# A two-block transformer on one core: modulation begun later, its sums kept in SBUF, activations saved in quarter tiles, side steps moved, four gate tiles

## The reference

```python
def _layer(x, ...):                      # first block, l = 0, 1
    proj = rms_norm(x, g_pre) @ w_in     # width 5952
    o_a = dense_attention(norm+rope(a_q), norm+rope(a_k), a_v) * silu(a_g)     # 8 heads of 128, 2 key heads
    o_b = dense_attention(q from norm(b_cq) @ w_uq, k, v from norm(b_ckv) @ w_ukv) * silu(b_g)   # 4 heads
    o_c = neighbourhood_attention(c_q, c_k, c_v, rpb) * silu(c_g)              # 4 heads, bias rpb
    return x + rms_norm(concat(o_a, o_b, o_c) @ w_out, g_post)

def hybrid_layer(x, c, ...):             # second block, l = 0, 1
    shift, scale, gate = split(silu(c) @ w_mod + b_mod)       # w_mod is 2048 x 6144
    h = rms_norm(x, g_pre) * (1 + scale) + shift
    a, s, g, z = split(h @ w_in)
    y = concat(sliding_window_attention(a), spatial_gating(s), gated_linear_attention(g)) * silu(z)
    return x + gate * rms_norm(y @ w_out, g_post)
```

## Time and profile before

| | |
|---|---|
| three runs | 3612.33, 3614.10, 3618.86 us (median 3614.1) |
| the profiled execution | 3606.72 us |
| its span in the profile | 3604.0 us |
| PE busy | 3484.3 us (97%), 17180 products |
| DVE busy | 1876.4 us (52%) |
| ACT busy | 1329.0 us (37%) |
| POOL busy | 1157.5 us (32%) |
| moved by DMA | 494.63 MB, 137 GB/s on average |
| PE on the chain that ended last | 83% |

### The profile page before, as it was taken

One profiled execution on the slowest core, in us unless ns is written; L12 is line 12 of the kernel. 1 busy time (PEld: TensorE's weight loads), 2 busy tenths in 40 slices (PEclk: granted clock), 3 DMA queues, 4 the chain that ended last, 5 costly groups with the idle time before them and its releaser, 6 DMA issues.

```text
span 3604.0 us, 47975 instructions
## 1 busy us (share of the span) xinstructions
PE 3484.3 (97%) x17180; PEld 2807.5 (78%) x17180; DVE 1876.4 (52%) x3156; ACT 1329.0 (37%) x2206; POOL 1157.5 (32%) x1244
## 2 busy tenths in 40 slices
PE   6999999999979999999999999999999999999998
PEld 5767878888766678788887878877887878877887
DVE  5633376543675334765436535645546535645545
ACT  5122323333541323333336535332236625423233
POOL 5664666664374546656620000002000000002000
PEclk9999999999989999999999999999999999999999
DMA  8644454455774444544556522322346622322345
GB/s 305 163 117 132 124 147 112 135 151 184 225 243 120 111 120 137 136 115 131 175 179 202 171 77 59 97 71 60 122 158 199 195 77 64 97 70 59 123 143 184
DMA packets 232384, 494.63 MB, mean 137 GB/s; under 512 B 36158, under 2 KB 45305, under 8 KB 226024
## 3 DMA queue, kind: packets, MB, share of 16 engines
q1 hardware_dynamic: 181352, 356.57, 32.8%
q0 software_dynamic: 33536, 109.10, 11.2%
q10 hardware_dynamic: 17280, 26.07, 2.3%
HBM read 470.58 MB, written 24.75 MB: 137 GB/s over the span
## 4 chain that ended last, share of the span: by engine, by line
PE 83%; DVE 8%; ACT 3%; DMA 3%; issue 2%; DVEq 0%; SPq 0%; ACTq 0%
PE bank L759 20%; PE bank L761 19%; PE bank L760 19%; PE bank L887 4%; PE bank L907 3%; DVE wlo L1699 2%; PE bank L873 2%; PE bank L754 2%; DMA stage<-in_w_out 2%; PE bank L756 2%; PE bank L755 2%; PE bank L896 2%; PE bank L1011 1%; DMA stage<-in_w_in 1%; PE bank L1143 1%
## 5 line engine op out<-in xcount | busy, mean ns | idle before, releaser
L759 PE MATMUL bank<-wlo,act_hi 128*128 128x512 f32 (+1 forms) x3712 | 1504.7, 405 | 71.4 <-DVE wlo L1699 60.4
L761 PE MATMUL bank<-whi,act_lo 128*128 128x512 f32 (+1 forms) x3712 | 1448.1, 390 | 0.0
L760 PE MATMUL bank<-whi,act_hi 128*128 128x512 f32 (+1 forms) x3712 | 1445.0, 389 | 0.0
L1699 DVE TENSOR_TENSOR wlo<-stage,whi 128x1024 fp32r<-128x1024 f32 (+1 forms) x624 | 831.3, 1336 | 880.8 <-ACT whi L1229 873.1
L1229 ACT ACTIVATE whi<-stage 128x1024 fp32r<-128x1024 f32 (+1 forms) x624 | 648.6, 1042 | 1029.2 <-PE bank L761 821.0
L759 PEld LDWEIGHTS bank<-wlo,act_hi 128*128 128x128 f32 x3712 | 702.9, 189 | 262.3 <-DVE wlo L1699 74.2
L761 PEld LDWEIGHTS bank<-whi,act_lo 128*128 128x128 f32 x3712 | 702.0, 189 | 148.8
L760 PEld LDWEIGHTS bank<-whi,act_hi 128*128 128x128 f32 x3712 | 704.2, 190 | 137.3 <-issue 7.7
L2648 POOL TENSOR_TENSOR macc<-macc,mprod 128x512 f32<-128x512 f32 x360 | 504.5, 1401 | 66.5 <-POOL mprod L2641 66.5
L2641 POOL TENSOR_SCALAR mprod<-wmod,csil 128x512 f32<-128x512 f32 x384 | 323.6, 843 | 378.7 <-DMA wmod<-in_w_mod 270.6
L2686 POOL DMA_DIRECT2D macc<-in_gla_w_gate_up x4 | 2.1, 528 | 1047.1 <-DVE Y L2297 1047.1
(11 more groups left out here) (259 smaller groups left out, 3222.6 us busy)
## 6 DMA issues: line engine op xcount, KB each, us to landing
stage<-in_w_in SPq DMA_DIRECT2D x400, 512.0 KB, 3.8
wmod<-in_w_mod POOLq DMA_DIRECT2D x384, 256.0 KB, 3.3
stage<-in_w_out SPq DMA_DIRECT2D x192, 512.0 KB, 4.1
out<-Y ACTq DMA_DIRECT2D x20, 1024.0 KB, 5.3
zone<-out SPq DMA_DIRECT2D x16, 1024.0 KB, 6.9
stage<-in_w_in SPq DMA_DIRECT2D x32, 320.0 KB, 4.0
Y<-in_x SPq DMA_DIRECT2D x4, 1024.0 KB, 13.7
rpb_tiles<-rpb_pad POOLq DMA_DIRECT2D x16, 224.0 KB, 5.9
```

Source lines behind the costliest of these rows:

```text
L759: pe.matmul(out, hi_x, lo_w, start=(k == 0), stop=False)
L760: pe.matmul(out, hi_x, hi_w, start=False, stop=False)
L761: mm = pe.matmul(out, lo_x, hi_w, start=False, stop=(k == KC - 1))
L1699: dve.tensor_tensor(wlo[:, c % RH, :, 0:width], stage[:, c % RS, :, 0:width], whi[:, c % RH, :, 0:width].bitcast(F32), ALU.subtract).then_ ...
```

## The change

1. **Modulation later.** In both layers POOL waits for the second increment of `prep` (the end of `key_rope_b`, step 36) before panel 0. Panels 0 and 1 now both stand ahead of the bias tiles. The sums of panels 0 to 3 move to steps 52, 62, 76 and 86 (`SUM_AT`; before 36, 52, 68, 84); those of panels 4 to 9 stay at steps 100 to 180, the last two at their places in the output sets. Attention units make room: branch B's 16 still end at step 68, branch C's begin at 81 (before 83) and end at 100 as before.
2. **Sums stay in SBUF.** `mrow` holds all 48 columns of both layers; ACT no longer writes to HBM at each sum. Shift and scale are used from there (`take_cols`); only the gate vectors go to HBM, by two DMAs of POOL, each 128 partitions by 16 numbers of 4 bytes (2048 numbers), when the first four head pairs of the sliding-window attention of the second block's first layer are done.
3. **Saves of x.** ACT saves no tile of x any more, except at the very end. SP saves in quarter tiles of 256 KB, one after each second weight cell, tile 0 in the last set of the layer before, tiles 1, 2, 3 in the layer's first, second and third set. The first layer saves nothing: its end reads `in_x`.
4. **w_uq and w_ukv in pieces.** SP loads `w_uq` in four DMAs in the fourth set and `w_ukv` in two in the fifth, in place of whole ones ahead of the third set.
5. **Start.** x's first tiles are loaded ahead of the small rows; ACT squares them ahead of the tangent of c, splits the first two weight cells ahead of the normalising, and normalises tile 0 while DVE normalises tile 1.
6. **Branch B's second latent** is squared and scaled in two halves (steps 24 and 33; before, both at 33). **Branch A's** key steps begin at 101 (before 107) and are spread to 112, its queries' to 113 to 122 and 134 to 148.
7. **Gates.** Four tiles in place of three, and DVE frees all four banks before it multiplies into Y.

```diff
-MOD_AT = {2: 0, 3: 1, 4: 2, 5: 3, 6: 4, 7: 5, 8: 6, 9: 7, 10: 8, 11: 9, 13: 10, 14: 11}
+MOD_AT = {6: 4, 7: 5, 8: 6, 9: 7, 10: 8, 11: 9, 13: 10, 14: 11}
-UNIT_TURN, UNIT_PV, ROW_SUM = 2, 4, 4
+UNIT_TURN, UNIT_PV = 2, 4
+SUM_AT = {52: 0, 62: 1, 76: 2, 86: 3} | {p * KC + 4: MOD_AT[p] for p in range(6, 12)}
-for first, steps in ((U_B, unit_steps(51, 16)), (U_C, unit_steps(83, 16))):
+for first, steps in ((U_B, unit_steps(51, 16)), (U_C, unit_steps(81, 16))):
+CKV0_AT = 24
-A_LOAD_AT, AK_AT, AQ_AT = 105, 107, (115, 131)
+A_LOAD_AT, AK_AT = 105, 101
+FOLD_AT, KROPE_AT = (112, 107), {108: 0, 109: 1, 110: 2, 111: 3}
+AQ_AT, ASUM_AT, ARSQ_AT = (113, 131), (116, 134), (122, 136)
+QROPE_A_AT = {113: (0, 0), 115: (0, 1), 119: (0, 2), 121: (0, 3), 139: (1, 0), 141: (1, 1), 146: (1, 2), 148: (1, 3)}
...
+            def x_save(blk, l, t, q):
+                def go():
+                    sp.wait_ge(x_new.sem, x_new.at(blk, l, t + 1 - TT))
+                    part = slice(q * PW, (q + 1) * PW)
+                    sp.dma_start(x_dram[:, t, part], Y[:, t, part]).then_inc(x_saved.sem, 16)
+                return go
...
-                in_set(0, l, 0, B_CQ0, first=4 if l == 0 else 0)
-                in_set(0, l, 1, B_CKV0, B_CKV_W)
-                sp.dma_start(wuq, io["b_w_uq"][bass.ds(l, 1)].rearrange("o (k p) n -> p (o k) n", p=P))\
-                sp.dma_start(wukv, io["b_w_ukv"][bass.ds(l, 1)].rearrange("o (k p) n -> p (o k) n", p=P))\
-                in_set(0, l, 2, B_CQ0)
-                in_set(0, l, 3, B_CKV0, B_CKV_W)
+                in_set(0, l, 0, B_CQ0, first=4 if l == 0 else 0, between=x_saves(0, l, 1))
+                in_set(0, l, 1, B_CKV0, B_CKV_W, between=x_saves(0, l, 2))
+                in_set(0, l, 2, B_CQ0, between=x_saves(0, l, 3))
+                in_set(0, l, 3, B_CKV0, B_CKV_W, between={2 * r + 1: w_uq(l, r) for r in range(4)})
...
             def mod_row_out(l, p):
                 act.wait_ge(mod_sum.sem, mod_sum.at(0, l, p + 1))
-                act.activation(mrow[:, :], MSUM[:, 0:PW // P], ACT.Copy).then_inc(mod_ev.sem, 1)
-                act.dma_start(mod_dram[bass.ds(l, 1), bass.ds(p * PW, PW)].rearrange("o (i c) -> c (o i)", c=P), mrow[:, :],
-                              allow_slow_non_contiguous=True).then_inc(mod_row.sem, 16)
+                act.activation(mrow[:, l, TT * p:TT * (p + 1)], MSUM[:, 0:PW // P], ACT.Copy).then_inc(mod_ev.sem, 1)
...
-                    gate(0)
-                    gate(1)
-                    apply(0)
-                    gate(2)
-                    apply(1)
-                    gate(3)
-                    apply(2)
-                    apply(3)
+                    for t in range(TT):
+                        gate(t)
+                    for t in range(TT):
+                        apply(t)
...
             for l in range(2):
-                pool.wait_ge(x_new.sem, x_new.at(0, l, -2))
+                pool.wait_ge(prep.sem, prep.at(0, l, CKV_READY + 1))
                 mod_panel(l, 0, 0)
+                mod_panel(l, 1, 1)
                 bias_tiles(l)
-                mod_panel(l, 1, 1)
...
+            pool.wait_ge(fin_done.sem, fin_done.at(1, 0, 4))
+            for l in range(2):
+                pool.dma_start(mod_dram[bass.ds(l, 1), :].rearrange("o (i c) -> c (o i)", c=P), mrow[:, l, 2 * KC:3 * KC],
+                               allow_slow_non_contiguous=True).then_inc(mod_row.sem, 16)
```

More of the change, by code:

```diff
@@ L60 @@
 U_B, U_C, U_A = 0, 16, 32
-UNIT_TURN, UNIT_PV, ROW_SUM = 2, 4, 4
+UNIT_TURN, UNIT_PV = 2, 4
+SUM_AT = {52: 0, 62: 1, 76: 2, 86: 3} | {p * KC + 4: MOD_AT[p] for p in range(6, 12)}
 GATED_STEPS = (2, 3, 4, 5, 6, 7, 8, 9, 10, 12, 14)
 def unit_steps(first, n, gates=False):
-    free = [s for s in range(first, first + 3 * n) if (s + UNIT_PV) % KC not in (ROW_SUM, ROW_SUM + 1)
+    free = [s for s in range(first, first + 3 * n) if s + UNIT_PV not in SUM_AT and s + UNIT_PV - 1 not in SUM_AT
             and (s < GATE0[0] * KC or not gates or s % KC in GATED_STEPS)]
@@ L437, in build, with sq_a @@
         tmp_a = view(ZT + 3584, 4, PW)
-        gate_tmp1 = [view(ZT + i * PW, PW) for i in range(3)]
+        gate_tmp1 = [view(ZT + i * PW, PW) for i in range(3)] + [view(ZV + 3 * PW, PW)]
+        def sq_a(half):
+            return (view(PP + 2048, 4, PW), tmp_a)[half]
         gain_at = ZK, ZT
@@ L563, in build @@
         gate_w, gate_b = macc[:, 0, 0:256], macc[:, 0, 256:512]
[L564 removed]
+        gate_tmp = (mprod[:, :], macc[:, 0, :], macc[:, 1, :], spare4[:, :])
         gsum, gmasks = view(PP, LEVELS + 2, P), view(PP + 1024, LEVELS + 2, P)
@@ L722, in _ @@
                 apart(sp)
-                spread(view(ZT, DM), mod_dram[one, 2 * DM:3 * DM], gain_in)
+                sp.wait_ge(mod_row.sem, mod_row.at(1, 2, 0))
+                apart(sp)
+                spread(view(ZT, DM), mod_dram[one, :], gain_in)
                 spread(view(ZV, DM), io["b_mod_2"][one, 2 * DM:3 * DM], gain_in)
```

246 lines of the change are left out of this document (137 added, 109 removed).

## The result

The changed kernel takes 3581.9 us (median of four runs, 3579.5 to 3584.1) against 3613.2 us (four runs of the kernel before, 3605.6 to 3618.9). The ratio is 0.9914, 95% interval 0.9894 to 0.9935: faster clear of the scatter, though by under 1%; 31 us by the medians, where the forecast had 16. The profiled execution is the one of 3579.51 us, 27.2 less than the profiled one before.

What follows compares the result with a forecast made beforehand. PE was taken as the bound, busy 97%, with only idle and half-clock time to win. Gains of 4 + 13 + 35 + 6 + 11 = 69 us less 53 us of waits for POOL gave -16: 3598 us, range 3562 to 3645.

Steps and rivals of the forecast that it cites:

- Start, 4: Kernel start to the first weight product: reordered splits, shared normalising and earlier x save 4 us (2 to 6).
- Steps 0 to 36, 13: First weight product to step 36 of layer 0: loads and saves leaving the DMA queues save 13 us (8 to 16).
- 890 to 1117, 35: End of layer 0 and start of layer 1: 35 of 45.8 us of idle and half-clock time go.
- Moved saves, part of 35 and 6: Layer and block borders: moved saves give part of both gains; by the shared-engines rule nothing, 5 us less in sum.
- Gates, 11: Gated panels: PE's waits for result banks that DVE frees late go, saving 11 us (7 to 11).
- POOL's lateness, 28 in layer 0: Layer 0 from step 36 to step 132: PE waits for POOL's late panels, costing 28 us.
- 25 in layer 1: Layer 1 up to step 132: the same lateness of POOL costs 25 us.
- Gate rows, chance 0.22, 3638: Second block's panel 3: two 2048-number writes block DMAs 80 us, PE waits 40, time 3638 us; chance 0.22.
- POOL keeps up: Rival: wait at step 86 shrinks to 5 us or none; 3533 at best, else 3565 us; chance 0.20.
- POOL behind more: Rival: loop panels take 64 us as late loads are not from row writes; 80 us in all, 3678; chance 0.08.
- the later borders: Between the blocks 5 us go through quarter saves and vanished row writes, 1 at the next border: 6 in all.

Runs made afterwards that it cites:

- e1: Changed kernel with one line undone: POOL begins modulation when two tiles of x are there, not at step 36; 3552.9 us, ratio 0.984.
- e6: Changed kernel with w_uq and w_ukv loaded as before, one behind the other ahead of the third set; 3594.7 us, ratio 0.996.
- e13: Changed kernel with early modulation, ACT's whole-tile saves, w_uq and w_ukv ahead of the third set and ACT's 24 row writes all put back; 3634.8 us, ratio 1.007.
- e3: Changed kernel with ACT's write of 512 numbers of 4 bytes put back behind each of the 24 sums; 3638.7 us, ratio 1.010.
- e4: Changed kernel with saves of x by ACT in whole tiles as before, layer 0 still saving nothing; 3581.2 us, ratio 0.992.
- e9: Changed kernel with POOL beginning modulation at the first increment of prep, 30 us earlier, not the second; 3526.9 us, ratio 0.978.
- e5: Changed kernel with the gates as before: three tiles, bank and Y multiplied in turn; 3598.0 us, ratio 0.998.
- e14: Changed kernel with modulation from prep's first increment, sums 3 to 7 at 88, 102, 119, 135, 150, and branch A's last query rotations moved; 3518.6 us, ratio 0.975.
- e12: The changed kernel as it is, measured again beside later runs; 3575.4 us, ratio 0.991.

## Why the forecast was right in direction and wrong in size

**Start, 4: right** (5.2; first weight product at 18.0 us, forecast of the first product 19). The order is the one forecast: ACT's two splits at 10.86 us, ahead of the normalising, and tile 1's share of that on DVE at 13.47.

**Steps 0 to 36, 13: right in size** (14.8) **and wrong in parts.** The term was reasoned from what leaves the DMA queues. In e1 modulation alone takes all of it back, and there DVE was late and no weight load was. w_uq's place costs 4.5 (e6) if it is undone; layer 0's saves were not tried; and with all put back the stretch is 9.3 us over the kernel before (e13), so the parts do not add up to the 14.8. That the size came out is in part luck.

**890 to 1117, 35: too small by 6**, the largest of the gains and one of the two failed steps. "Of 45.8 us I leave 11, what the stretch at 1870 shows today": the rest in the stretch at 1870 was no floor. It was itself under the row writes: in e3 ACT waits 13.6 us there for loads of w_out (16.7 in the kernel before, none in the change), PE 5.0 us for late cells (7.2 and 1.5), and the time from the last sum to the end is 3.8 us longer. What the change left at the border is 2.3 us of idle time at full clock. The reason behind the term was off too: most of what modulation costs at the border came through DVE, by e1's trace, and 8.8 us have no cause shown.

**Moved saves, part of 35 and 6: nothing** (e4: 3581.2 against 3581.9, border 1.9 us). The rule weighed there, several queues feed the same 16 engines and moving only saves issue time (the Trainium skill, "Trainium Kernel Development and Optimization", Key Constraints), agrees with these runs for the saves. It does not speak of work moved in time on its own queue, such as modulation: 30 us earlier than in the change it costs nothing (e9), from the start of the layer 14.8 and 19.9 us (e1).

**Gates, 11: too small as a price** (14, e5; the upper bound was 11) **and not there in the sum.** The forecast had branch A's spread steps as a gain only. Two rotations now stand on DVE in front of the last unit ahead of the first gated panel, and the wait there grew from 0.44 to 1.94 us in layer 0, with 3.4 us of half clock. e14 shows the wait shrink when they are moved. Between sum 6 and the last sum only 1.5 us a layer were left.

**POOL's lateness, 28 in layer 0: right** (29.3), and its parts: first product 9.4 us behind step 36 (forecast 9), panel 3 done 250.9 behind it (251), wait at step 86 20.90 (22), at step 132 3.1 (9); but 5.1 at step 116 where I had 0.4, since panel 5 took 60.7 us, not 56. The total is nearer than its parts, which missed both ways (and the forecast's own step 132 should read 426.0, not 425.7). **25 in layer 1: 7 too much**, the other failed step. Panel 3 ended 243.7 us behind step 36, 7.2 sooner than in layer 0, where I took 2.8: panel 2 took 53.9 us there in place of 56.6, and the pause with the bias tiles 14.8 (from 1196.47 to 1211.31) where layer 0 had 18.8 and I had taken 16.9, measured once in the kernel before. PE waited 13.7 us at step 86 (forecast 19), and 13.4 in e12.

These two, -6 and -7, make 13 of the 10 us between -26 and -16; the other terms give 3 back, gates and the later borders above all. The 4 us between the medians' difference (31.4) and the profiled executions' (27.2) lie within the scatter of the runs.

**Gate rows, chance 0.22, 3638: did not happen, though it began to.** The two writes go out at 2129.32, and the weight load issued at 2135.57, 5 us behind the second, lands 17.4 us after its issue, the next one after 9.5. All engines from 2134 to 2150 us, and then the DMA view of 2133 to 2151 (count, size and median us to landing of the loads issued there; 3.7 is their usual time):

```profile
2134.00:2150.00 16.00, 15.75 (x98) 13.03 (x98) 7.01 (x24) 7.34 (x19) 0.00 (x0) 1.00 0.57 18
```

```profile
stage<-in_w_in SPq DMA_DIRECT2D x2, 512.0 KB, 13.5
```

For 16 us the DMA engines move 18 GB/s, and SP's two loads are held up. That is a block of 14 us for 4096 numbers, where 512 through ACT's queue block for 8 to 10: far from eight times as long, and within the 40 us in hand. The chance was too high; the sentence against it ("what blocks may be numbers that share a line, not their count") pointed the right way, without being shown. **POOL keeps up** did not happen (its 3565 us leaves out the 12 us of branch A that its 3533 has; with them it is 3553), **POOL behind more** neither; e3 shows that something like it, with panels of 58 to 66 us, is what the change would have met with its row writes left in. The step that made the forecast's 55.5 to 60 us panels out of the earlier trace rows was right.

## What to carry to other kernels

Before moving a background stream out of the way of a tight stretch, count what its consumer needs from the new start, piece by piece; the wait that comes is as certain as the gain. Then look for a place between the two: 30 us of shift kept the whole gain and left 6.8 us of waits, which neither end of the range did. Look for it in every engine's row, not in the DMA queues alone: here the stream's arithmetic on POOL lengthened DVE's instructions, and that shows in DVE's busy time for the same count of instructions. Small results that would be written out as scattered 4-byte numbers, beside a stream that is on the path, are better kept in SBUF: 24 such writes were worth 57 us here.

## What was not expected of the hardware

A row write is about one packet for each number on ACT's queue: its packets go from 2304 to 14976 when the 24 writes come back (e3), 528 for 512 numbers. The Trainium skill, page "DMA: Bandwidth & Descriptors", section "Rules for kernel authors", says of a non-contiguous last dimension that it becomes one descriptor per element, which agrees. On POOL's queue the two gate-row writes, 4096 numbers, added 96 packets in all (33536 to 33632 for its queue in the profile), landed in 5.0 and 6.1 us, and yet kept the next weight loads out until 23.7 us after the first of them. That is far from one packet for each number; which of queue and shape made the difference was not tried.

DVE is slower beside a working POOL: up to step 36, 93.4 us for 159 instructions against 69.5 (e1 and the change), and instructions on two columns take up to 1.28 us in place of 0.17. A DMA share of 0.58 with POOL idle lengthens none of the change's splits.

The costs of four edits, 30.6 us in sum, gave 32.5 together at the border, though they came through DVE for one and through late loads for another. And in layer 1 with POOL on the path the same wait at step 86 was 13.4 to 13.7 us in the change and 17.1 to 20.9 in kernels that changed other things (e4, e5, e6), so single waits of this size should not be forecast to better than 5 us.
